# Two of six conditioning parts made by GpSimd beside the second mixers, with x1 resting in DRAM meanwhile

## What is computed

```python
def reference(x, ...):
    x = first_block(x, ...)                    # h @ w_in, mixers, @ w_out, + hier_moe
    return second_block(x, c, ...)

def second_block(x, c, ...):
    mod = silu(c) @ w_ada + b_ada              # six parts of 2048
    sh1, sc1, g1, sh2, sc2, g2 = split(mod, 6)
    h = rms_norm(x, mix_norm_pre) * (1 + sc1) + sh1
    ... = split_cols(h @ w_in)                 # hgrn2, dilated attention, convolution
    merged = sigmoid(h @ w_gate + b_gate) * (each mixer @ its w_out), summed
    x = x + g1 * rms_norm(merged @ w_o, mix_norm_post)
    h = rms_norm(x, mlp_norm_pre) * (1 + sc2) + sh2
    x = x + g2 * rms_norm(relu(h @ w_up)**2 @ w_down, mlp_norm_post)
```

## Time and profile before

| | us |
|---|---|
| median of 3 runs | 3133.31 |
| the runs | 3134.56, 3130.65, 3133.31 |
| profiled execution, its own time | 3129.2 |
| its span in the trace | 3127.3 |
| PE busy | 2975.1 (95%) |
| DVE busy | 2145.3 (69%) |
| ACT busy | 1517.1 (49%) |
| POOL busy | 261.6 (8%) |

### The profile page before, as it was taken

The page is one execution under the profiler, slowest core; times in us unless marked ns, Lnnn a source line. Parts: engine busy times, 40 slices in busy tenths (PEclk is TensorE's granted clock), DMA queues, the critical chain, the costliest instruction groups (busy, mean ns, idle before and its releaser), DMA issues. The chain is left out here.

```text
span 3127.3 us, 43200 instructions
## 1 busy us (share of the span) xinstructions
PE 2975.1 (95%) x17313; PEld 2440.1 (78%) x17313; DVE 2145.3 (69%) x2430; ACT 1517.1 (49%) x1860; POOL 261.6 (8%) x134
## 2 busy tenths in 40 slices
PE   8899889997999999998999999999997999999997
PEld 8889867875776677876788878878786888888886
DVE  6778775456899877766468868745667666666666
ACT  5345451234777755554344475555444444444443
POOL 0000002000000000000000000000003333233320
PEclk9999999998999999998999999999999999999999
DMA  8988856287999978772677745664765666666663
GB/s 299 304 283 258 286 229 232 102 333 271 341 378 350 362 258 273 256 254 73 215 224 220 235 154 163 218 225 149 275 217 181 204 215 217 215 201 215 215 229 107
DMA packets 362745, 737.98 MB, mean 236 GB/s; under 512 B 20469, under 2 KB 118882, under 8 KB 353231
## 3 DMA queue, kind: packets, MB, share of 16 engines
q1 hardware_dynamic: 348036, 713.20, 66.8%
q10 hardware_dynamic: 14540, 22.43, 2.0%
HBM read 708.93 MB, written 26.65 MB: 235 GB/s over the span
## 5 line engine op out<-in xcount | busy, mean ns | idle before, releaser
L301 DVE TENSOR_TENSOR moe_w_lo<-ring,moe_w_hi 128x1024 fp32r<-128x1024 f32 x384 | 457.8, 1221 | 132.2 <-ACT moe_w_hi L291 127.6
L301 DVE TENSOR_TENSOR mx_w_lo<-ring,mx_w_hi 128x1024 fp32r<-128x1024 f32 (+1 forms) x288 | 346.9, 1210 | 279.6 <-ACT mx_w_hi L291 276.1
L291 ACT CAST moe_w_hi<-ring 128x1024 fp32r<-128x1024 f32 x384 | 395.4, 1048 | 246.6 <-PE psum L317 241.5
L301 DVE TENSOR_TENSOR mlp_w_lo<-ring,mlp_w_hi 128x1024 fp32r<-128x1024 f32 x256 | 322.5, 1261 | 263.8 <-ACT mlp_w_hi L291 263.8
L291 ACT CAST mx_w_hi<-ring 128x1024 fp32r<-128x1024 f32 (+1 forms) x288 | 296.6, 1036 | 420.5 <-PE psum L317 402.5
L291 ACT CAST mlp_w_hi<-ring 128x1024 fp32r<-128x1024 f32 x256 | 268.1, 1049 | 403.8 <-PE psum L317 403.8
L317 PE MATMUL psum<-mx_w_hi,mx_a_hi 128*128 128x496 f32 (+1 forms) x1024 | 405.9, 396 | 5.2 <-DVE mx_w_lo L301 3.7
L317 PE MATMUL psum<-mx_w_hi,mx_a_lo 128*128 128x496 f32 (+1 forms) x1024 | 398.4, 389 | 0.0
L317 PE MATMUL psum<-mx_w_lo,mx_a_hi 128*128 128x496 f32 (+1 forms) x1024 | 398.2, 389 | 0.0
L317 PE MATMUL psum<-in_w_hi,in_a_hi 128*128 128x314 f32 x768 | 245.8, 320 | 11.8 <-DVE in_w_lo L301 11.7
L317 PE MATMUL psum<-in_w_hi,in_a_lo 128*128 128x314 f32 x768 | 238.8, 311 | 0.0
(11 more groups left out here) (630 smaller groups left out, 5736.3 us busy)
## 6 DMA issues: line engine op xcount, KB each, us to landing
ring<-in_w_ada SPq DMA_DIRECT2D x64, 1024.0 KB, 8.5
ring<-in_w_e_gate SPq DMA_DIRECT2D x64, 1024.0 KB, 5.8
ring<-in_w_e_up SPq DMA_DIRECT2D x64, 1024.0 KB, 6.7
ring<-in_w_e_down SPq DMA_DIRECT2D x64, 1024.0 KB, 6.3
ring<-in_w_up SPq DMA_DIRECT2D x64, 1024.0 KB, 5.2
ring<-in_w_down SPq DMA_DIRECT2D x64, 1024.0 KB, 5.1
ring<-in_w_in SPq DMA_DIRECT2D x64, 992.0 KB, 5.7
ring<-in_w_in SPq DMA_DIRECT2D x96, 628.0 KB, 6.3
```

The costliest lines, as they stand in the source:

```text
L291: self.nc.scalar.copy(self.w[0][:, self._half(j, half), :, 0:cols], self.view[:, slot, ks, 0:cols]).then_inc(self.hi_done, 1)
L301: self.nc.vector.tensor_tensor(self.w[1][:, q, :, 0:cols], self.view[:, j % self.slots, ks, 0:cols], self.w[0][:, q, :, 0:cols].bitcast(F3 ...
```

## The change

- **first_stream** makes part 0 alone: 32 units rather than 64, unit u at tick 9 + 3u (three ticks apart; 2.2 before), none beyond tick 102.
- **rwkv** makes part 1 with the same 16 products, and issues the same 24 loads.
- **mix_output** makes the first half of part 2 with its 8 products at the start. The 8 products beside its chunks go, with their loads. SP now issues x and the next four conditioning loads ahead of the ninth chunk of w_out.
- **normed_parts** makes the second half of part 2; **route** makes none.
- **experts** reads three parts back, and loads b_ada's parts 3 and 4 straight to where the sums will be added.
- **second_mixers** gets the class LateModulation for parts 3 and 4. SP saves what is needed of x1 (1.25 MB, 4 DMAs) into unused rows of `proj1`, then loads 128 units of 128x512 (256 KB) into two tiles, one in the room of x1; unit u waits until GpSimd has spent unit u - 2. GpSimd multiplies and adds each unit into a total that lies in x1's room (248 instructions). PE sums the totals with 16 small matmuls at tick 108 and 16 at tick 228, DVE adds them into `modc`, and SP loads x1 back after tick 232. The loads of units 0 to 63 stand at ticks 4 to 98, those of 64 to 127 at ticks 110 to 204.
- **feed_forward** stays as it is.

```diff
@@ -615,3 +615,3 @@
 
-    SPARE = 32
+    SPARE = 16
 
@@ -630,3 +630,3 @@
     def spare_tick(self, u):
-        return 9 + 11 * u // 5 if u < 43 else 131 + 2 * (u - 43)
+        return 9 + 3 * u
 
@@ -913,3 +913,3 @@
                 ada.begin()
-                ada.load(sp, 56)
+                ada.load(sp, 40)
                 sp.wait_ge(prod, 10)
@@ -1220,3 +1220,3 @@
 
-                pe.wait_ge(ada.copied, 3)
+                pe.wait_ge(ada.copied, 2)
                 pe.wait_ge(v_ready, 1)
...
@@ -1335,16 +1334,13 @@
                     b, c = ORDER_OUT[j]
-                    if j == spare:
+                    if j == x_at:
                         sp.wait_ge(turned, 4)
                         sp.dma_start(x1[:], d["x"][0].rearrange("(t p) n -> p t n", p=P)).then_inc(x_in, 16)
+                        for s in range(FEW, RING):
+                            ring.load(sp, s, next_weights(0, s), ring.loads[s] + 1)
                     ring.load(sp, j % FEW, weights(0, b * KC + c), ring.loads[j % FEW] + 1,
                               split_out=split.out_of_ring(j - FEW) if j >= FEW else None)
-                    if j < spare:
-                        s = spare_slot(j)
-                        ring.load(sp, s, ada.source(0, j), ring.loads[s] + j // FEW + 1)
+                for s in range(FEW):
+                    ring.loads[s] += body // FEW
+                    ring.load(sp, s, next_weights(0, s), ring.loads[s] + 1, split_out=split.last_in(s))
                 for s in range(RING):
-                    ring.loads[s] += (body if s < FEW else spare) // FEW
-                ada.loaded += spare
-                for s in (4, 5, 6, 7, 0, 1, 2, 3):
-                    ring.load(sp, s, next_weights(0, s), ring.loads[s] + 1,
-                              split_out=split.last_in(s) if s < FEW else None)
                     ring.loads[s] += 1
@@ -1374,6 +1370,2 @@
                               c * KC, c == 0, c == KC - 1)
-                    if j < spare:
-                        s = spare_slot(j)
-                        pe.wait_ge(ring.full[s], 16 * (ring.uses[s] + j // FEW + 1))
-                        ada.product(pe, ada.used + j, ring.buf[:, s]).then_inc(ring.free[s], 1)
 
@@ -1396,7 +1388,3 @@
                     split.part_hi(q)
-                hi(5, spare + 3)
-                s = spare_slot(spare - 1)
-                sc.wait_ge(ring.free[s], ring.uses[s] + spare // FEW + 1)
-                ada.row_out(sc)
-                hi(spare + 3, body)
+                hi(5, body)
 
...
@@ -1492,3 +1477,2 @@
                 inputs.load(sp)
-                ada.load(sp, 80)
 
@@ -1608,3 +1592,2 @@
                 mm.then_inc(turned, 1)
-                ada.use(pe, 3)
 
@@ -1618,6 +1601,5 @@
                                  stop=True).then_inc(counted, 1)
-                ada.use(pe, 5)
 
                 pe.wait_ge(slotted, 1)
-                pe.wait_ge(ada.copied, 5)
+                pe.wait_ge(ada.copied, 3)
                 pe.wait_ge(y_left, T)
...
@@ -1852,5 +1834,7 @@
                 chunk = expert_chunk(sp, rt, source)
-                sp.wait_ge(ada.stored, 16 * 5)
-                sp.dma_start(mod_rows, d["mod"][0:1, 0:5 * D].rearrange("a (r p) -> (a r) p", p=P)).then_inc(mod_in, 16)
-                sp.dma_start(mod_bias, d["b_ada_2"][:, 0:5 * D].rearrange("a (r p) -> (a r) p", p=P)).then_inc(mod_in, 16)
+                by_col = lambda a: a.rearrange("a (r p) -> (a r) p", p=P)
+                sp.wait_ge(ada.stored, 16 * 3)
+                sp.dma_start(mod_rows[0:n_sum], by_col(d["mod"][0:1, 0:3 * D])).then_inc(mod_in, 16)
+                sp.dma_start(mod_rows[n_sum:n_mod], by_col(d["b_ada_2"][:, 3 * D:5 * D])).then_inc(mod_in, 16)
+                sp.dma_start(mod_bias, by_col(d["b_ada_2"][:, 0:3 * D])).then_inc(mod_in, 16)
                 ring.rest(sp, chunk, 1, body, split)
@@ -2044,4 +2028,4 @@
                 def mod_sum():
-                    ve.wait_ge(mod_in, 32)
-                    step(nc.vector.tensor_tensor(mod_rows, mod_rows, mod_bias, ALU.add))
+                    ve.wait_ge(mod_in, 48)
+                    step(nc.vector.tensor_tensor(mod_rows[0:n_sum], mod_rows[0:n_sum], mod_bias, ALU.add))
 
@@ -2051,5 +2035,4 @@
                     ve.sem_inc(mod_made, 1)
-                    for part, name in ((1, "mix_norm_pre_2"), (4, "mlp_norm_pre_2")):
-                        g, c0 = modc[:, part * KT:(part + 1) * KT], CC[name][0]
-                        step(nc.vector.scalar_tensor_tensor(g, g, 1.0, chip.cols[:, c0:c0 + KT], ALU.add, ALU.mult))
+                    g, c0 = modc[:, KT:2 * KT], CC["mix_norm_pre_2"][0]
+                    step(nc.vector.scalar_tensor_tensor(g, g, 1.0, chip.cols[:, c0:c0 + KT], ALU.add, ALU.mult))
 
@@ -2960,2 +2943,93 @@
 
+class LateModulation:
+    PARTS, UNITS = (3, 4), 2 * KT * (D // NB)
+    BEGIN, AGAIN, SUM, LAST, BACK = 4, 110, (54 * 2, 114 * 2), (110, 230), 232
+    def __init__(self, chip, st, x1, modc, norm, tile):
+        self.chip, self.x1, self.modc, self.norm = chip, x1, modc, norm
+        self.total, self.tiles = x1[:, 0], (x1[:, 1, 0:NB], tile)
+        free = chip.dram["proj1"][1:1 + S, GATES * NB:IN1].rearrange("(t p) n -> t p n", p=P)
+        room, w = IN1 - GATES * NB, D // 2
+        self.kept = [(x1[:, 0, 0:w], free[0, :, 0:w]), (x1[:, 0, w:D], free[1, :, 0:w]),
+                     (x1[:, 1, 0:room - w], free[0, :, w:room]),
+                     (x1[:, 1, room - w:NB], free[1, :, w:w + NB - (room - w)])]
+        self.sums = (chip.psum[:, 0, W2:W2 + KT], chip.psum[:, 6, 0:KT])
+        self.saved, self.spent, self.pooled, self.summed, self.dve, self.taken, self.back = (
+            st.sem(f"late_{n}") for n in ("saved", "spent", "pooled", "summed", "dve", "taken", "back"))
+        self.filled = [st.sem(f"late_filled{n}") for n in range(2)]
+    def unit(self, u):
+        part, rest_ = divmod(u, self.UNITS // 2)
+        k, b = divmod(rest_, D // NB)
+        return part, k, b
+    def tick(self, u):
+        half = self.UNITS // 2
+        return (self.BEGIN if u < half else self.AGAIN) + 3 * (u % half) // 2
+    def sync(self, sp):
+        w = self.chip.dram["w_ada_2"][0]
+        yield 1
+        for here, there in self.kept:
+            sp.dma_start(there, here).then_inc(self.saved, 16)
+        for u in range(self.UNITS):
+            part, k, b = self.unit(u)
+            at = self.PARTS[part] * D + b * NB
+            yield self.tick(u)
+            if u == 0:
+                sp.wait_ge(self.saved, 64)
+                sp.wait_ge(self.norm.scaled, T * KC)
+            if u >= 2:
+                sp.wait_ge(self.spent, u - 1)
+            sp.dma_start(self.tiles[u % 2], w[k * P:(k + 1) * P, at:at + NB]).then_inc(self.filled[u % 2], 16)
+        yield self.BACK
+        sp.wait_ge(self.summed, 2)
+        for here, there in self.kept:
+            sp.dma_start(here, there).then_inc(self.back, 16)
+    def pool(self, po):
+        nc, step, c0 = self.chip.nc, Steps(po, self.pooled), CC["c_2"][0]
+        po.wait_ge(self.saved, 64)
+        po.wait_ge(self.norm.scaled, T * KC)
+        for u in range(self.UNITS):
+            part, k, b = self.unit(u)
+            c, x, total = self.chip.cols[:, c0 + k:c0 + k + 1], self.tiles[u % 2], self.total[:, b * NB:(b + 1) * NB]
+            if part and k == b == 0:
+                po.wait_ge(self.summed, 1)
+            po.wait_ge(self.filled[u % 2], 16 * (u // 2 + 1))
+            if k == 0:
+                step(nc.gpsimd.tensor_scalar(total, x, c, None, ALU.mult))
+            else:
+                step(nc.gpsimd.tensor_scalar(x, x, c, None, ALU.mult))
+                step(nc.gpsimd.tensor_tensor(total, total, x, ALU.add))
+            po.sem_inc(self.spent, 1)
+    def tensor(self, pe, evicted, da):
+        for n in range(2):
+            yield self.SUM[n]
+            pe.wait_ge(self.spent, (n + 1) * self.UNITS // 2)
+            if n == 0:
+                pe.wait_ge(evicted, self.SUM[n] // 2 // KC)
+            else:
+                pe.wait_ge(da.ov_left, len(da.items))
+            for k in range(KT):
+                mm = self.chip.nc.tensor.matmul(self.sums[n][:, k:k + 1], self.total[:, k * P:(k + 1) * P],
+                                                self.chip.c("ones")[:, 0:1], start=True, stop=True)
+            mm.then_inc(self.summed, 1)
+    def vector(self, ve):
+        nc, step = self.chip.nc, Steps(ve, self.dve)
+        part = lambda n: self.modc[:, n * KT:(n + 1) * KT]
+        for n, p in enumerate(self.PARTS):
+            yield self.LAST[n]
+            ve.wait_ge(self.summed, n + 1)
+            nc.vector.tensor_tensor(part(p), part(p), self.sums[n], ALU.add).then_inc(self.taken, 1)
+            ve.wait_ge(self.taken, n + 1)
+        g, c0 = part(4), CC["mlp_norm_pre_2"][0]
+        step(nc.vector.scalar_tensor_tensor(g, g, 1.0, self.chip.cols[:, c0:c0 + KT], ALU.add, ALU.mult))
 def gate_rows(d, g):
...
@@ -3065,2 +3140,7 @@
```

(17 more changed lines are left out.)

18 lines of the change are left out of this document (9 added, 9 removed).

## The result

| | before | after |
|---|---|---|
| median (5 runs each) | 3132.41 us | 3148.23 us |
| span of the profiled execution | 3127.3 | 3143.2 |
| ratio | | 1.0051, 95% interval 1.0036 to 1.0066 |

A forecast was written before the change was run, and what follows sets the result against it. PE, busy 95% of the span, was taken as the bound. The terms -20.9 - 6.1 + 0 + 7.2 + 9 + 5 + 1 summed to -4.8 us, giving a median of 3128.5 us, with a range of 3108 to 3163.

The forecast's parts named there:

- rival 4: In second_mixers DVE is the bound, 1.3 us a unit and upper bounds +21 and +15: 3150.5 us; chance 0.06.
- first_stream, -20.9: Halving first_stream's units from 64 to 32 saves 18.8 us and PE's fewer sums 2.1; bounds -10.5 and -25.9.
- SP's queue and the loads behind it: In first_stream SP's queue stands 193.7 us at L641 waiting for DVE, the chunk's load behind it, holding the stream back.
- Rival 3: first_stream was not held by the units, so the -18.8 us falls away: 3147.3 us; chance 0.10.
- mix_output, -6.1: In mix_output eight products and their loads go, of which five count: 6.1 us saved; bounds -9.8 and -3.
- route and the rest, 0: Changes in rwkv, normed_parts, route and experts together cost or save nothing; bounds -3 and +1 us.
- PE's sums, +7.2: In second_mixers two sums of 16 one-column matmuls cost PE 3.6 us each; bounds +3.6 and +12.
- x1, +1: Saving x1 to DRAM and back in second_mixers costs 1 us; bounds 0 and +3.
- Beside the convolution, +9: In second_mixers GpSimd takes 0.9 us a unit from DVE, 28.8 for 32 units, mostly absorbed; bounds 0 and +21.
- the dense rows: Profile rows where two DVE instructions took 3.45 us beside GpSimd's addition, 2.76 beside its multiplication: 1.3 us a unit.
- Beside the recurrence and the attention, +5: In second_mixers eight units at 0.9 us, 60% on the chain, cost 4 us, and one more elsewhere; bounds 0 and +15.
- rival 5: An engine blocks the other for whole instructions, each unit taking 2.86 us from DVE: 3200 us; chance 0.05.

The follow-up runs named there:

- e11_units_not_added: The kernel before without DVE's 60 multiply-adds of conditioning units in first_stream, all 64 loads and SP's waits kept: 3108.0 us, ratio 0.9924.
- e2_loads_only: The changed kernel without GpSimd's multiplications and additions; all DMAs, SP's waits, x1's save and return and PE's sums kept: 3102.2 us, ratio 0.9901.
- e1_no_late: The changed kernel without anything of LateModulation (no x1 save or return, units or sums; parts 3 and 4 are b_ada alone): 3095.1 us, ratio 0.9879.
- e7_not_beside_conv: The changed kernel with GpSimd doing nothing for units 32 to 63, loads, waits and the other 96 units kept: 3121.0 us, ratio 0.9962.
- e5_add_only: The changed kernel without GpSimd's multiplications, except the 8 first ones; 120 additions stay: 3128.0 us, ratio 0.9985.
- e8_halved_add: The changed kernel with each of GpSimd's 128x512 additions cut into two of 128x256: 3145.8 us, ratio 1.0040.
- e10_loads_no_sums: The changed kernel without GpSimd's arithmetic and with one matmul rather than 16 in each of PE's two sums: 3097.8 us, ratio 0.9895.

## Why the prediction was wrong

The step that failed is the price of GpSimd's work in second_mixers: 0.9 us of DVE's time a unit beside the convolution, where it was 1.35, and eight units that count beside the recurrence and the attention, where 53 took DVE's time. What happened is nearest to rival 4, which had 0.06: DVE the bound in second_mixers, 1.3 us a unit, 3150.5 worked out and 3148.2 measured. That the two lie 2 us apart is in part luck: rival 4 kept a gain in first_stream that was 8 us too small, and its costs in second_mixers were too small by nearly as much. Point by point, from the traces:

- **first_stream, -20.9: measured -29.2,** past the bound of -25.9, though not past the -43.9 named as the utmost. The term that was mis-sized is the stretch 280 to 378. I took 12.6, the middle between a count by idle time and one by matmuls; from chunk 68 to the end of the stage 20.3 us went. The spread of the other 11 units was put at 6.2 and gave 6 to 9. The reasoning "SP's queue and the loads behind it" was the smaller part, 8.5 us: with all loads kept, e11_units_not_added gained 20.7 us by leaving out DVE's 1.28 us a unit, which I had called worth nothing by itself. In the stretch 280 to 378 the two halves are about equal. Rival 3 is refuted.
- **mix_output, -6.1: measured -6.1** (-34.9 against -28.8), with one wait where the prediction put it and one elsewhere.
- **route and the rest, 0: measured +0.4** up to mix_output **and -1.3** between mix_output and second_mixers, within the bounds.
- **PE's sums, +7.2 and x1, +1: measured 7.1** by the medians of e2_loads_only and e1_no_late and 10.6 in their traces. The matmuls last 3.6 us a sum, as forecast. But 11.4 us go at the first sum and nothing that shows at the second, where the forecast had 3.6 twice, and x1's way nothing that shows; the wait behind the first sum was not in the forecast.
- **Beside the convolution, +9: measured +24,** against the loads alone (chunk 54 is 27.9 us later, chunk 60 24.1). The mechanism was right and the terms of its sum were off. Most went wrong where I chose 0.9 us a unit, between an average over feed_forward and the dense rows: the dense rows' 1.3 was right, 1.35 as measured. The average of 0.12 is that of a DVE with 263.8 us of idle time, and was no guide to one without. Next, I counted 32 units and it was 37 in the window, or 34 that begin beside the convolution itself, which starts at chunk 25, ahead of unit 32. (The units kept the places of their ticks: unit 32 begins in chunk 26 and unit 63 in chunk 50.) So DVE got 50.1 us more work and not 28.8. Its idle time took 19.0 of it, a little more than the 14.4 counted. Of the 31 us left 24 reached the stream behind chunk 54, so DVE's lead and the slack behind the convolution took 7, near the 5.7 counted. In e7_not_beside_conv the 32 units were worth 27.3 us by the medians, 24.3 in the trace.
- **Beside the recurrence and the attention, +5: measured 17** (chunks 60 to 100 take 294.4 us in the change and 277.7 with the loads alone). The price a unit was too high here and the number of units far too low. The same 1351 matmuls, first before and then in the change:

```profile
1816.60:2094.30 277.70, 271.89 (x1351) 222.55 (x1351) 197.41 (x187) 163.27 (x168) 0.00 (x0) 0.99 0.58 195
1815.80:2110.30 294.50, 273.54 (x1351) 222.72 (x1351) 233.77 (x187) 163.32 (x168) 189.28 (x105) 0.99 0.68 230
```

  DVE is busy 36.4 us longer for 53 units, 0.69 each, and 17 of it reached the end. I had counted eight units, those between 1820 and 1850 where PE waited in the trace of before, and one more us for all others. Chunks 60 to 80 lost 11.2 us and chunks 80 to 100 another 5.5; which instructions carry the loss there was not resolved.
- **The Trainium skill's rule** for the shared port ("SBUF — State Buffer", section "Who interferes with whom"), rival 5: the addition agrees with it in part, 0.96 to 1.02 us of its 1.29. The multiplication does not, 0.28 to 0.30 of 1.57. By the rule, as rival 5 reads it, a unit would have taken 2.86 us from DVE; it took 1.35.

The decision between 0.12 and 1.3 carried the whole sign. With 1.3 in place of 0.9 the forecast's own sum has 32 x 1.3 - 14.4 - 5.7 = 21.5 us beside the convolution in place of 9, and gives 3141: slower than before. What is left to 3148.2 are the other terms above, which went both ways.

## What to carry to other kernels

An engine that is idle is free only for as long as what it disturbs has idle time in that stretch: price GpSimd's work by how much of it touches VectorE there, in stretches, and put it where VectorE pauses. Here 64 units cost 2 us in one place and 32 units 24 to 27 us in another. Count the units over the whole stretch, not only where the trace of before has its waits. Take a contention figure from the densest place of the trace when the target is dense; an average over a stretch with pauses hides it. And costs that share one slack don't add in time until the slack is gone: 6 and 26 made 46 by the medians, 1 and 23 made 41 in the traces.

## What the runs showed of the hardware

- GpSimd's addition of 128x512 (two inputs in SBUF) takes 0.96 to 1.02 us from a VectorE that is busy with two-input instructions, its multiplication (one input) 0.28 to 0.30; the ranges come from counting all 36 in the window or the 34 that begin beside the convolution. Cut into halves, the addition costs the same in sum (1.3 us a unit, where 1.35 was the whole).
- What a unit takes from VectorE grows with how busy VectorE is (what VectorE runs differs between these stretches too, so the two are not told apart). By VectorE's busy time before and after it is (66.51 - 58.79) for about 26 units, 0.3 us, where VectorE was busy 46% (1448 to 1576); 0.69 us where it was busy 71% (chunks 60 to 100); and 1.35 where it was busy 89%, beside the convolution.
- In the change the added time lands on the short instructions: three of 128x256 in a row took up to 2.66 us where they took 1.27, and the 1.18 us low part right behind did not stretch. A piece of DVE's timeline in the change:

```profile
1649.23 2.66 DVE L2517 SCALAR_TENSOR_TENSOR actT<-ring,actT 128x256 f32<-128x256 f32 x3
1651.81 1.18 DVE L301 TENSOR_TENSOR mx_w_lo<-ring,mx_w_hi 128x992 fp32r<-128x992 f32 x1
1652.91 2.29 DVE L2517 SCALAR_TENSOR_TENSOR actT<-ring,actT 128x256 f32<-128x256 f32 x3
```

- It is not always so: with additions alone the low parts stretched too, to 1.27 us on average, and with halved additions to 1.33 (e5_add_only, e8_halved_add).
- GpSimd is slowed as well: beside the convolution its multiplication takes 2.06 us (1.57 at its shortest in the trace of before) and its addition 1.70 (1.29).
- The loads of the units alone, without GpSimd's arithmetic, raised the DMA share from 0.70 to 0.83 ahead of the convolution (e2_loads_only, 1448 to 1576), and chunk 54 came after 301.7 us rather than 301.5. All that loads, waits and x1's way cost is 2.7 us by the medians, 4.7 in the traces (e10_loads_no_sums), and it falls between chunks 54 and 60, where the first sum is.
